# The second layer's expert stage as a stream over all experts, in place of gathers

## The reference, cut to what matters

```python
def chunk(xc):                                   # 128 tokens at a time
    q = (xc @ w_q).reshape(PEER_CHUNK, PEER_HEADS, 2, PEER_HALF)
    s = jnp.einsum('thid,hikd->thik', q, sub_keys)
    s1, i1 = lax.top_k(s[:, :, 0], PEER_TOPK)    # 16 of 128 keys
    s2, i2 = lax.top_k(s[:, :, 1], PEER_TOPK)
    ...                                          # the 16 best sums of 16 x 16
    eidx = jnp.take_along_axis(cidx, pos, axis=-1)   # i1 * 128 + i2
    gate = jax.nn.softmax(top_s, axis=-1)
    u = u_emb[eidx]
    hid = jax.nn.gelu(jnp.einsum('td,thkd->thk', xc, u))
    wgt = gate * hid
    return jnp.einsum('thk,thkd->td', wgt, v_emb[eidx])
```

## Time and profile before

| what | value |
|---|---|
| device time, median of 3 runs | 3652.65 us (3651.92 to 3653.02) |
| span of the profiled execution (nothing longer is given for it) | 3762.1 us |
| instructions | 31263 |
| mean granted TensorE clock, share of full speed | 0.913 |
| HBM read, written | 1120.20 MB, 8.46 MB |
| `peer10`, from its first turned tile 1 token to its last sum | 2577 to 3344.6 us |

### The profile page before, as it was taken

How to read it: one execution, slowest core, us unless ns; L and a number is a source line. 1 busy time by engine, 2 the same in 40 slices (tenths; PEclk the granted TensorE clock), 3 DMA queues, 4 the chain that set the end, 5 groups by cost and what they waited for, 6 DMA issues and landing times.

```text
span 3762.1 us, 31263 instructions
## 1 busy us (share of the span) xinstructions
PE 3071.3 (82%) x11602; PEld 1350.9 (36%) x11602; DVE 1966.2 (52%) x4453; ACT 367.3 (10%) x935; POOL 1538.7 (41%) x1584
## 2 busy tenths in 40 slices
PE   7999888688989878678878788887566666689999
PEld 4484446233533325323323223446111111125444
DVE  0051457677666644666666534455666666513223
ACT  1000321020000001000000001230000000002212
POOL 0010004556656654566666661003566666630000
PEclk9999998789999989889889899998978888899999
DMA  6274238889999997899999997527899999973242
GB/s 271 106 289 167 85 133 335 322 286 389 412 395 401 390 410 277 341 412 400 412 412 412 405 412 277 208 80 292 353 365 368 356 366 361 371 291 124 102 157 79
DMA packets 261506, 1130.78 MB, mean 301 GB/s; under 512 B 29796, under 2 KB 37188, under 8 KB 242280
## 3 DMA queue, kind: packets, MB, share of 16 engines
q0 software_dynamic: 221184, 805.40, 55.3%
q1 hardware_dynamic: 35496, 315.97, 21.5%
q10 hardware_dynamic: 4672, 7.41, 0.5%
HBM read 1120.20 MB, written 8.46 MB: 300 GB/s over the span
## 4 chain that ended last, share of the span: by engine, by line
PE 42%; DVE 21%; DMA 17%; POOL 7%; issue 6%; another core or an unknown queue 5%; ACT 2%; SPq 0%; DVEq 0%; ACTq 0%; POOLq 0%
DVE big L2568 9%; PE ps L1064 8%; PE ps L2375 7%; DMA big<-in_u,xT 7%; DMA big<-in_v,xT 6%; POOL big L2612 6%; PE ps L242 6%; PE ps L2290 3%; PE ps L724 1%; DMA w<-in_w_in 1%; DMA bc<-in_w_mod 1%; PE ps L1759 1%; PE ps L1616 1%; PE ps L1183 1%
## 5 line engine op out<-in xcount | busy, mean ns | idle before, releaser
L2375 PE MATMUL ps<-big,bc 128*32 128x512 f32 x3072 | 1050.9, 683 | 368.4 <-DMA big<-in_v,xT 265.5
L2568 DVE CUSTOM_DVE_ANT_0 big<-big,ps 128x1024 f32<-128x1024 f32 x768 | 920.5, 1214 | 304.0 <-DMA big<-in_u,xT 231.3
L2612 POOL DMA_INDIRECT big<-in_u,xT x768 | 731.6, 953 | 619.0 <-issue 194.2
L2612 POOL DMA_INDIRECT big<-in_v,xT x768 | 734.1, 956 | 405.5 <-issue 203.8
L2375 PEld LDWEIGHTS ps<-big,bc 128*32 128x32 f32 x3072 | 192.7, 117 | 1103.3 <-issue 544.9
L1064 PE MATMUL ps<-w,xT 128*128 128x512 f32 x768 | 339.8, 599 | 6.1 <-DMA w<-in_w_in 3.2
L242 PE MATMUL ps<-w,xT 128*128 128x512 f32 x512 | 223.8, 597 | 2.8 <-ACT xT L521 1.2
L1064 PEld LDWEIGHTS ps<-w,xT 128*128 128x128 f32 x768 | 145.6, 192 | 184.4 <-issue 175.7
L2290 PE MATMUL ps<-tmp,w 128*128 128x256 f32 (+1 forms) x832 | 183.4, 381 | 21.1 <-issue 18.2
L2290 PEld LDWEIGHTS ps<-tmp,w 128*128 128x128 f32 x832 | 154.6, 207 | 47.4 <-issue 26.2
L592 POOL TENSOR_TENSOR small<-small 128x32 f32<-128x32 f32 (+1 forms) x8 | 33.2, 4155 | 299.3 <-DVE small L563 239.0
(11 more groups left out here) (371 smaller groups left out, 3094.1 us busy)
## 6 DMA issues: line engine op xcount, KB each, us to landing
w<-in_w_in SPq DMA_DIRECT2D x58, 2048.0 KB
bc<-in_w_mod SPq DMA_DIRECT2D x20, 2048.0 KB, 10.6
w<-in_w_conv SPq DMA_DIRECT2D x24, 1536.0 KB
w<-in_peer_wq SPq DMA_DIRECT2D x12, 2048.0 KB
w<-in_w_out SPq DMA_DIRECT2D x10, 2048.0 KB
w<-in_conv_out_w SPq DMA_DIRECT2D x6, 2048.0 KB
big<-in_u,xT POOLq DMA_INDIRECT x768
big<-in_v,xT POOLq DMA_INDIRECT x768
```

What stands on the lines that cost most here:

```text
L2375: ins = pe.e.matmul(self.ps[32 * g:32 * g + 32, 2 + half, :], p["diag"][part % 2][:, 256 * g + 32 * m:256 * g + 32 * m + 32], p["ring"][:, ...
L2568: dve.inc(dve.e.tensor_tensor_reduce(out=row, in0=row, in1=p["xc"], scale=1.0, scalar=0.0, op0=ALU.mult, op1=ALU.add, accum_out=p["hid"][t ...
L2612: ins = pool.e.indirect_dma_start(p["ring"][:, slot, :], None, table, bass.IndirectOffsetOnAxis(index, 0))
```

## The change

Layer 1's expert stage is replaced (`dense_*` for `peer_*` where l is 1). Both tables are stored by the host in 64 blocks ("pairs" of second keys), `u_blocks` turned for TensorE and `v_blocks` by rows, 1 MB each. The stage reads each once, in order. The first half multiplies every pair of `u` with all 256 tokens (`block`: 16 products of 256 columns), and ScalarE copies the result out of PSUM. The first 60 results are stored in DRAM (`hidden`, 256 KB each) and the last four stay in SBUF. Meanwhile VectorE makes two one-hot tables for four tokens at a time (`dense_hot_dve`, the gate within the first), and TensorE multiplies them (`mass`: 4 products of 128 columns) into a table of gates over all 128 x 128 keys for each token, which ScalarE copies into `mass` (64 KB a partition for a tile; one in `big`, one in the new `arena`, in which `h`, `xT`, `bb` and `bc` lie too). The second half reads the hidden values back, takes the gelu of all of them (ScalarE: square and tanh, VectorE: two operations), multiplies them into the gates in place, and sums with the `v` pairs (`summed`: 8 products of 512 columns). There are no gathers in this stage any more. The routing drops its three operations on expert numbers and reads its scores from SBUF.

In the second block one gain row is loaded later, and tile 1 is turned behind the second product, not the first. The bias table's loads move behind the first half.

```diff
+        arena = sb("arena", 18 * D)
+        self.h = arena[:, 0:4 * D].rearrange("p (a d) -> p a d", a=4)
...
+        self.bb = arena[:, 8 * D:12 * D]
+        self.bc = arena[:, 12 * D:18 * D].rearrange("p (a d) -> p a d", a=6)
...
+        self.mass = [self.big[:, :, :].rearrange("p a n -> p (a n)").rearrange("p (b t) -> p b t", t=P),
+                     arena[:, 2 * D:18 * D].rearrange("p (b t) -> p b t", t=P)]
...
+    def dense_order(self):
+        scored = {0: 4, 1: 5, 4: 6, 7: 7, 10: 8, 13: 9, 15: 10, 17: 11, 31: 12, 34: 13, 37: 14, 40: 15}
+        turned, spread = {18: 0, 47: 1}, {0: 19, 1: 48}
+        order = []
+        for n in range(4, 20):
+            order.append(("query", n))
+            if n in (9, 19):
+                order.append(("scores", 2 if n == 9 else 3))
+        for pair in range(PAIRS):
+            if pair in scored:
+                order.append(("scores", scored[pair]))
+            if pair in (42, 46):
+                order.append(("gates", 14 + pair // 46))
+            if pair in turned:
+                order.append(("turn", turned[pair]))
+            for block in range(2):
+                order.append(("block", 2 * pair + block))
+                for tile, first in spread.items():
+                    if first <= pair < first + 8:
+                        at = 32 * tile + 4 * (pair - first) + 2 * block
+                        order += [("half", at), ("half", at + 1)]
+        return order
+    def dense_sums(self):
+        return [60, 61, 62, 63, *range(60)]
...
+        sums = self.dense_sums()
+        for n in range(4):
+            sp.wait_ge(self.pe, name, "q", last(2 + n // 2))
+            self.stream_in[n].inc(sp.e.dma_start(self.quarter(n), self.d["u_blocks"][n]), name, "u in", n)
+        for n in range(PAIRS):
+            sp.wait_ge(self.pe, name, "hidden", n)
+            if n + 4 < PAIRS:
+                self.stream_in[n % 4].inc(sp.e.dma_start(self.quarter(n), self.d["u_blocks"][n + 4]), name, "u in", n + 4)
+            else:
+                at = n + 4 - PAIRS
+                self.stream_in[n % 4].inc(sp.e.dma_start(self.quarter(n), self.d["v_blocks"][sums[at]]), name, "v in", at)
+            if n < 60:
+                sp.wait_ge(self.act, name, "hid", n)
+                self.hid_out[n % 4].inc(sp.e.dma_start(self.d["hidden"][n], p["hid"](n)), name, "hid out", n)
+        self.load_row(sp, 0, self.mod_row(1, 0)(5), name, "gate", dst=p["gate_row"])
+        self.load_row(sp, 1, self.d["norm_g_2"][0:1, :], "norm2nd0", 0, dst=self.gain2(0))
+        for at in range(PAIRS):
+            if at + 4 < PAIRS:
+                sp.wait_ge(self.dve, name, "gelu", at)
+                sp.wait_ge(self.hid_out[sums[at + 4] % 4], name, "hid out", sums[at + 4])
+                self.hid_in[at % 4].inc(sp.e.dma_start(p["hid"](at), self.d["hidden"][sums[at + 4]]), name, "hid in", at + 4)
+            if at + 4 < 60:
+                sp.wait_ge(self.pe, name, "summed", at)
+                self.stream_in[at % 4].inc(sp.e.dma_start(self.quarter(at), self.d["v_blocks"][sums[at + 4]]), name, "v in", at + 4)
+            if at == 2:
+                sp.wait_ge(self.pe, name, "mass", HALVES - 1)
+                self.bias_turned_sp(sp)
+            if at in (24, 32, 40, 48):
+                late = (at - 24) // 8
+                self.late_in[late].inc(sp.e.dma_start(self.late(late), self.d["v_blocks"][sums[60 + late]]), name, "late in", late)
+        self.w_release[0], self.w_release[1] = (name, "summed", 57), (name, "summed", 59)
...
+        def tables_turned(tile):
+            pe.wait_ge(self.dve, name, "gates", 8 * tile + 7)
+            if tile:
+                pe.wait_ge(self.act, name, "mass out", 15)
+            for a in range(3):
+                src = p["picked"][tile][:, a, :] if a < 2 else p["gates"][tile]
+                ins = pe.e.transpose(self.ps[:, 2, a * P:(a + 1) * P], src, self.ident[:, :])
+            pe.inc(ins, name, "tables", tile)
+        def block(b):
+            pair, at = b // 2, b % 2
+            if not at:
+                pe.wait_ge(self.stream_in[pair % 4], name, "u in", pair)
+                if pair >= 3:
+                    pe.wait_ge(self.act, name, "hid", pair - 3)
+                if pair == 2:
+                    pe.wait_ge(self.act, name, "q out", 19)
+            w = self.quarter(pair).rearrange("p (b k i) -> p b k i", b=2, k=KC)
+            for k in range(KC):
+                ins = pe.e.matmul(self.ps[:, self.block_bank(pair), at * SEQ:(at + 1) * SEQ], w[:, at, k, :], p["xT"][:, k, :],
+                                  start=k == 0, stop=k == KC - 1)
+            if at:
+                pe.inc(ins, name, "hidden", pair)
+        def mass(n):
+            group = n // 2
+            pe.wait_ge(self.dve, name, "hot", n)
+            if group >= 2:
+                pe.wait_ge(self.act, name, "mass out", group - 2)
+            for j in range(4):
+                ins = pe.e.matmul(self.ps[:, self.group_banks(group) + n % 2, j * P:(j + 1) * P], p["rows"](n)[:, j, :], p["cols"](n)[:, j, :],
+                                  start=True, stop=True)
+            pe.inc(ins, name, "mass", n)
...
+        def summed(at, tiles, first, last):
+            pair = sums[at]
+            w = (self.quarter(at) if at < 60 else self.late(at - 60)).rearrange("p (b n) -> p b n", b=2)
+            for b in range(2):
+                for tile in tiles:
+                    for half in range(2):
+                        ins = pe.e.matmul(self.ps[:, 2 * tile + half, :], self.mass[tile][:, 2 * pair + b, :], w[:, b, half * BANK:(half + 1) * BANK],
+                                          start=first and not b, stop=last and b == 1)
+            return ins
+        for g in (30, 31):
+            pe.wait_ge(self.act, name, "mass out", g)
+        pe.wait_ge(self.act, name, "hid", PAIRS - 1)
+        for at in range(60):
+            pe.wait_ge(self.stream_in[at % 4], name, "v in", at)
+            pe.wait_ge(self.dve, name, "weighed", at)
+            pe.inc(summed(at, range(2), not at, False), name, "summed", at)
+        for tile in range(2):
+            for at in range(60, PAIRS):
+                pe.wait_ge(self.late_in[at - 60], name, "late in", at - 60)
+                pe.wait_ge(self.dve, name, "weighed", at)
+                ins = summed(at, [tile], False, at == PAIRS - 1)
+            pe.inc(ins, name, "sum", tile)
...
+        def hidden(pair):
+            act.wait_ge(self.pe, name, "hidden", pair)
+            if pair >= 4:
+                act.wait_ge(self.hid_out[pair % 4], name, "hid out", pair - 4)
+            act.inc(act.e.copy(p["hid"](pair), self.ps[:, self.block_bank(pair), :]), name, "hid", pair)
+        def mass(group):
+            tile, first, bank = group // 16, group % 16 * 8, self.group_banks(group)
+            act.wait_ge(self.pe, name, "mass", 2 * group + 1)
+            src = self.ps[:, bank:bank + 2, :].rearrange("p a n -> p (a n)").rearrange("p (t b) -> p b t", t=8)
+            act.inc(act.e.copy(self.mass[tile][:, :, first:first + 8], src), name, "mass out", group)
...
+        def square(at):
+            if at < 4:
+                act.wait_ge(act, name, "hid", self.dense_sums()[at])
+            else:
+                act.wait_ge(self.hid_in[at % 4], name, "hid in", at)
+            if at >= 2:
+                act.wait_ge(self.dve, name, "weighed", at - 2)
+            act.inc(act.e.activation(p["act"](at), p["hid"](at), ACT.Square), name, "square", at)
+        square(0)
+        for at in range(PAIRS):
+            if at + 1 < PAIRS:
+                square(at + 1)
+            act.wait_ge(self.dve, name, "inner", at)
+            act.inc(act.e.activation(p["act"](at), p["act"](at), ACT.Tanh, scale=CUBE * ROOT), name, "tanh", at)
...
+    def dense_hot_dve(self, dve, name, p, n):
+        tile, first = n // 32, n % 32 * 4
+        dve.wait_ge(self.act, name, "tables out", tile)
+        if n >= 2:
+            dve.wait_ge(self.pe, name, "mass", n - 2)
+        for j in range(4):
+            t = first + j
+            dve.inc(dve.e.tensor_scalar(p["rows"](n)[:, j, :], p["key"], p["table"](tile, 0)[:, t:t + 1], p["table"](tile, 2)[:, t:t + 1],
+                                        ALU.is_equal, ALU.mult))
+        picked = p["table"](tile, 1)[:, first:first + 4].unsqueeze(2).broadcast_to((P, 4, P))
+        dve.inc(dve.e.tensor_tensor(p["cols"](n), p["key"].unsqueeze(1).broadcast_to((P, 4, P)), picked, ALU.is_equal), name, "hot", n)
+    def dense_weights_dve(self, dve, name, p):
+        def inner(at):
+            dve.wait_ge(self.act, name, "square", at)
+            dve.inc(dve.e.scalar_tensor_tensor(out=p["act"](at), in0=p["act"](at), scalar=1.0 / CUBE, in1=p["hid"](at), op0=ALU.add, op1=ALU.mult),
+                    name, "inner", at)
+        inner(0)
+        for at, pair in enumerate(self.dense_sums()):
+            if at + 1 < PAIRS:
+                inner(at + 1)
```

(34 more changed lines are left out.)

258 lines of the change are left out of this document (227 added, 31 removed).

## The result

| what | before | after |
|---|---|---|
| device time, median of 4 runs each | 3652.84 us (3651.92 to 3657.33) | 3964.78 us (3955.26 to 3968.38) |
| span of the profiled execution | 3762.1 us | 3953.7 us |
| mean granted TensorE clock | 0.913 | 0.954 |
| last expert stage, turn of tile 1 to the first turn of the second block | 767 us there, 690 us in two later profiles | 1007 us |

The change makes the kernel slower: ratio 1.0846, with a 95% interval from 1.0826 to 1.0865. The forecast was 3462 us with 0.96 on faster; the time lies 503 us above it and outside the range.

What follows compares the result with a forecast made beforehand. The prediction took the old stage to be bound by its gathers' bytes and the new one by TensorE, its last sum ending at 3128 us of the profiled span instead of 3344.6; 3652.65 - 190 = 3462 us, range 3430 to 3525.

Steps and rivals of the forecast that it cites:

- TensorE's new work: TensorE's products in the new stage: 3.54 us a pair in the first half, 3.46 in the second, some 510 us in all.
- The sum: Whole kernel: old stage 735 us outside the profiler, 183 to 210 us to be had, 190 taken, giving 3462 us.
- Between the halves: Between first and second half, TensorE idles until copy, square, inner, tanh, gelu and gate products are through: 4.5 us.
- VectorE in the first half: VectorE's routing steps at 10.0 us and gate tables at 1.9 us a half, pacing TensorE within the two groups.
- rival of cheaper tables: VectorE's small compares overlap, a half of a gate table costs 1.45 us, the kernel takes 3433 us; chance 0.08.
- The second half: Three close rates a pair: TensorE 3.46 us, VectorE and ScalarE chain 3.2, DMA stream 3.06 to 3.35; TensorE sets 221.7 us.
- The end: After the last sum: tile 0's residual and norm (some 6 us) and the second block's weight chunks are hidden, costing nothing.
- Starved of instructions: TensorE in the new stage waits for 15 instruction fetches at 5 us each, 75 us, giving 3537 us; chance 0.12.
- Stream or gelu chain: Second half paced by gelu chain (3.7 us a pair) or stream (3.63), giving 3475 to 3485 us; chance 0.2.
- Half clock: Waits keep TensorE at 1.2 GHz, 510 us of work becomes 1020, the kernel takes 3943 us; chance 0.03.

Runs made afterwards that it cites:

- u_half: The changed kernel with half of each u product left out (8 products of 256 columns a pair in place of 16): 3756.56 us, ratio 1.0286.
- both_half: As u_half, and the second half sums only one of a pair's two blocks (4 products of 512 columns in place of 8): 3551.33 us, ratio 0.9722.
- bf16: The changed kernel with the products of both streamed halves in bfloat16, tables still float32 in DRAM: 3561.39 us, ratio 0.9745.
- before_again: The kernel before, unchanged, profiled a second time: 3652.99 us, with a span of 3651.7 us.
- before_third: The kernel before, unchanged, run a third time, on a third chip: 3652.33 us.
- bf16_late_b: The bf16 kernel with hidden values copied out before the next u pair is rounded, and v rounded one pair ahead, not two: 3514.45 us, ratio 0.9612.

## Why the prediction was wrong, step by step

**"TensorE's new work", the price of a product, is the step that failed.** I read "32 products of 128 columns took 3.73 us" from the earlier trace rows, and likewise 48 and 48 from the earlier trace rows. The counts in those rows are matmul instructions of the trace, and a float32 product leaves two. The rows held 16, 24 and 24 products: 0.233, 0.443 and 0.865 us each. Every term doubles, or nearly:

| term | forecast | measured |
|---|---|---|
| queries | 25 us | 51 (16.39 + 34.70) |
| first half, a pair | 3.54 us | 7.07 (6.9 from start to start) |
| gate tables | 30 us | 62 |
| second half, a pair | 3.46 us | 6.9 (442 / 64) |
| the stage | 551 us | 1007 |

The work is a little under twice 510 us, since the prices above hold each group's tail. The 36 us of waits for VectorE's tables that I had added did not come: nothing at L2784 is waited for. The stage is 456 us longer than forecast, and that explains 456 of the 503 us. u_half and both_half showed that this work is the stage, and bf16 that the price belongs to float32: a product of 512 columns starts 0.215 us behind the last in bfloat16 (2934.47 - 2934.04 for two) and takes 0.865 us in float32. At 2.4 GHz that is one cycle a column against four, worked out from these rows. Beside this the Trainium skill, "FP8 and Floating Point Precision", section "TensorE Precision Notes", says that true float32 takes four passes through the array; the rows agree with it. By that rule my estimate for 256 columns would have been 4 x 256 / 2.4 GHz = 0.427 us, near the 0.443 measured. I had not set the rows' counts against the program's, although both stood ahead of the prediction: four products for two slots, and the earlier trace rows.

**"The sum", the old stage, was mis-sized by 45 us.** I took 190 us to be had from 735 us outside the profile. before_again and before_third have 690 us. Against my 551 us for the new one only 139 us were to be had, 51 less than I took, and the forecast should have been 3514. (That bf16_late_b took 3514 us as well is chance: other engines and the stream set its stage.) The two errors, 456 and 51, make 507 us, 4 more than the 503 to be explained.

**"Between the halves"**: 4.5 us forecast, 4.3 measured (the wait for L2994).

**"VectorE in the first half"**: two halves of a gate table took 3.26 us, 1.63 each, where I had 1.9; VectorE's timeline of the changed kernel in one group of halves:

```profile
2729.05 1.11 DVE L2971 TENSOR_SCALAR merged<-mrow,merged 128x128 f32<-128x128 f32 x4 [7.24 <-PE ps L2784]
2730.07 0.68 DVE L2974 TENSOR_TENSOR merged<-mrow,merged 128x512 f32<-128x512 f32 x1
2730.68 1.11 DVE L2971 TENSOR_SCALAR merged<-mrow,merged 128x128 f32<-128x128 f32 x4
2731.70 0.68 DVE L2974 TENSOR_TENSOR merged<-mrow,merged 128x512 f32<-128x512 f32 x1
2734.28 1.11 DVE L2971 TENSOR_SCALAR merged<-mrow,merged 128x128 f32<-128x128 f32 x4 [1.90 <-PE ps L2784]
```

The four compares overlap (1.11 us for four whose own records are 0.34 each), so the half came out between mine and the 1.45 of the rival of cheaper tables. It gained nothing here: VectorE waits 1.9 us for TensorE after each two, since TensorE needs 5.2 us for the products between them (2734.28 - 2729.05). ScalarE's copies of 1024 columns took 1.01 us, priced at 1.06.

**"The second half"**: the stream was rightly sized, and the chain a little long. They show only where TensorE is cheap: in bf16_late_b a pair takes 3.42 us in the mean, with 3.24 for its bytes (I had 3.06 to 3.35), and the chain takes 2.97 where I had 3.2, even with the rounding of `v` in its queues. TensorE's 3.46 us was the rate of nothing. In both_half, at the price that I had assumed, a pair took 3.8 us (245 / 64), with waits for the hidden values' reads that I had not priced.

**"The end"** held: from the last sum to the second block's first product 1.76 us, as before, and no late chunk.

**The rivals.** *Starved of instructions* is refuted: TensorE was busy 200 of 200 us with the DMA share at 0.49 to 0.57. By the same error it counted 15 fetches, where the stage's 3900 rows make some 31 (an estimate from the whole kernel's 28,080 matmul and weight load rows in 111 fetches). *Stream or gelu chain* did not happen, since TensorE paces both halves with the DMA engines half idle. *Half clock* had given 3943 us, near the 3965 that came, by luck, for a cause that was not there: the granted clock was 0.99 to 1.00. It put 2 x 510 us into the stage by another route, and the time alone would have seemed to prove it; the clock column rules it out.

## What to carry to other kernels

Before a row of a timeline becomes the price of an operation, set its count against the number of operations that the program issues there: one division would have turned this forecast round. In float32 a product cost four times one in bfloat16 here, so trading gathered bytes for products wants that price first: here 268 MB of gathers (690 us) were beaten only once the streamed products were in bfloat16 (3514 us, ratio 0.961), and the old kernel stood better than the float32 stream by 8%. In a program that an engine runs in order, an operation placed early to be ready early can hold up all behind it: two such orders undone gave 49 us here, together.

## What the runs showed of the hardware

- A float32 product is two matmul rows in the trace: 2048 rows for 1024 products, 7.07 us for 16 of 256 columns. In bfloat16 it is one row: 1024 for 1024.
- TensorE without a pause for 200 us had a granted clock of 1.00 in one stretch and 0.99 in another. In the second half of bf16_late_b, busy 121.56 of 200 us in bursts, it was 0.93 in the mean. After a wait of 4.77 us in its first half, behind other waits, the lower level shows: 16 bfloat16 products of 256 columns took 3.60 us, and the next 16 took 1.93. TensorE's timeline, and the granted clock (the number before the last two) of two stretches in them:

```profile
2666.86 3.60 PE L2801 MATMUL ps<-merged,w 128*128 128x256 bf16 x16 [4.77 <-ACT w L2693]
...
2670.89 1.93 PE L2801 MATMUL ps<-merged,w 128*128 128x256 bf16 x16
```

```profile
2667.00:2670.00 3.00, 3.00 (x15) 2.13 (x14) 2.75 (x15) 2.09 (x2) 0.00 (x0) 0.50 0.89 325
2671.00:2673.00 2.00, 1.82 (x17) 1.37 (x15) 1.86 (x8) 0.32 (x1) 0.00 (x0) 1.00 0.71 193
```

- Loads of 1 MB and reads of 256 KB streamed at 404 GB/s on one core, as the gathers of 4 KB rows did (400 to 403).
- The same program took 3652 us on most occasions and 3774 on one chip. Its gathers were seen at 361 and at 400 GB/s, in profiles with a span of 3762 and 3652 us. The stage that streams instead of gathering took 550 us in one and 553 in the other of two chips, and did not show this.
